# Low parts of the query units and every other quad's second ones by GpSimd; the first half of the selection under the query projection

## What is computed

```python
def peer(x, w_query, sub_keys, expert_down, expert_up):
    ...
    q = (xt @ w_query).reshape(T, PEER_HEADS, 2, PEER_HALF)
    scores = jnp.einsum('thpc,hpnc->thpn', q, sub_keys).astype(jnp.float32)
    vals, idx = lax.top_k(scores, PEER_TOPK)
    cand = (vals[..., 0, :, None] + vals[..., 1, None, :]).reshape(T, PEER_HEADS, PEER_TOPK * PEER_TOPK)
    top_vals, top_c = lax.top_k(cand, PEER_TOPK)
    i1 = jnp.take_along_axis(idx[..., 0, :], top_c // PEER_TOPK, axis=-1)
    i2 = jnp.take_along_axis(idx[..., 1, :], top_c % PEER_TOPK, axis=-1)
    experts = (i1 * PEER_N_KEYS + i2).reshape(T, PEER_HEADS * PEER_TOPK)
    ...
        u = jnp.take(expert_down, ec, axis=0)
        hdn = jax.nn.gelu(jnp.einsum('ted,td->te', u, xc))
        vsel = jnp.take(expert_up, ec, axis=0)
        return jnp.einsum('te,ted->td', gc * hdn, vsel)
```

## Time and profile before

| | us |
|---|---|
| median of 3 runs | 2942.48 (2939.5 to 2945.15) |
| profiled execution | 2936.86 |
| its span | 2935.1 |
| PE busy | 2811.8 (96%) |
| DVE busy | 2050.6 (70%) |
| ACT busy | 1118.3 (38%) |
| POOL busy | 542.0 (18%) |

### The profile page before, as it was taken

One profiled execution on the slowest core, in us unless ns is written; L12 is line 12 of the kernel. 1 busy time (PEld: TensorE's weight loads), 2 busy tenths in 40 slices (PEclk: granted clock), 3 DMA queues, 4 the chain that ended last, 5 costly groups with the idle time before them and its releaser, 6 DMA issues.

```text
span 2935.1 us, 40591 instructions
## 1 busy us (share of the span) xinstructions
PE 2811.8 (96%) x15985; PEld 2275.7 (78%) x15985; DVE 2050.6 (70%) x3115; ACT 1118.3 (38%) x1743; POOL 542.0 (18%) x534
## 2 busy tenths in 40 slices
PE   6999999999999999899999999999999989999997
PEld 4788888887879988798897799888888877444443
DVE  4688877778765456744655669985559999666666
ACT  3344444445454445644455542112027986000000
POOL 1000000000000000000000002334435457544443
PEclk9999999999999999999999999999999999999999
DMA  9988888887866635365443646999998888999997
GB/s 362 361 288 271 270 269 269 270 268 269 294 201 179 174 112 167 124 201 170 136 130 122 202 135 231 351 339 409 407 356 284 295 295 322 408 409 409 409 409 319
DMA packets 345757, 799.55 MB, mean 272 GB/s; under 512 B 40104, under 2 KB 95648, under 8 KB 344800
## 3 DMA queue, kind: packets, MB, share of 16 engines
q1 hardware_dynamic: 270576, 505.70, 50.6%
q0 software_dynamic: 74992, 291.27, 26.4%
HBM read 794.76 MB, written 2.10 MB: 271 GB/s over the span
## 4 chain that ended last, share of the span: by engine, by line
PE 67%; DMA 14%; DVE 6%; ACT 5%; issue 4%; POOL 4%; SPq 0%; DVEq 0%; ACTq 0%; POOLq 0%
PE ps L2042 16%; PE ps L2044 15%; PE ps L2043 15%; PE ps L2607 13%; DMA s<-in_up_rows,s 12%; POOL s L735 3%; DVE s L1995 2%; DVE r L1268 1%; ACT s L1185 1%; DMA s<-in_down_rows,s 1%; DMA s<-in_ret_first 1%; DVE s L1976 1%; ACT s L1155 1%; ACT s L1163 1%; PE ps L2342 1%
## 5 line engine op out<-in xcount | busy, mean ns | idle before, releaser
L2042 PE MATMUL ps<-r,r 128*128 128x256 f32 (+1 forms) x2976 | 999.9, 336 | 14.8 <-DVE r L1268 12.4
L2044 PE MATMUL ps<-r,r 128*128 128x256 f32 (+1 forms) x2976 | 980.1, 329 | 0.0
L2043 PE MATMUL ps<-r,r 128*128 128x256 f32 (+1 forms) x2976 | 979.3, 329 | 0.0
L1268 DVE TENSOR_TENSOR r<-s,r 128x1024 fp32r<-128x1024 f32 (+2 forms) x532 | 640.1, 1212 | 418.9 <-ACT r L750 417.0
L750 ACT CAST r<-s 128x1024 fp32r<-128x1024 f32 (+2 forms) x532 | 549.0, 1039 | 740.2 <-PE ps L2044 696.8
L2042 PEld LDWEIGHTS ps<-r,r 128*128 128x128 f32 x2976 | 569.0, 191 | 81.0 <-issue 21.2
L2043 PEld LDWEIGHTS ps<-r,r 128*128 128x128 f32 x2976 | 569.3, 191 | 52.6 <-issue 5.3
L2044 PEld LDWEIGHTS ps<-r,r 128*128 128x128 f32 x2976 | 568.3, 191 | 50.5
L2732 PE MATMUL ps<-s,big 128*128 128x512 f32 x1024 | 441.6, 594 | 1.5 <-DMA s<-in_up_blocks 1.5
L1995 DVE SCALAR_TENSOR_TENSOR s<-s,s,s 128x1024 f32<-128x1024 f32 x256 | 328.8, 1284 | 162.3 <-DMA s<-in_up_rows,s 160.6
L1976 DVE CUSTOM_DVE_ANT_0 s<-s,s 128x1152 f32<-128x1152 f32 x256 | 345.6, 1352 | 97.3 <-DMA s<-in_down_rows,s 97.1
(11 more groups left out here) (315 smaller groups left out, 2244.1 us busy)
## 6 DMA issues: line engine op xcount, KB each, us to landing
s<-in_ada_w SPq DMA_DIRECT2D x128, 512.0 KB, 5.5
s<-in_up_blocks SPq DMA_DIRECT2D x128, 512.0 KB
s<-in_ret_w_in SPq DMA_DIRECT2D x112, 512.0 KB, 5.3
s<-in_down_blocks SPq DMA_DIRECT2D x128, 448.0 KB
s<-in_w_in SPq DMA_DIRECT2D x96, 512.0 KB, 3.9
s<-in_ret_w_out SPq DMA_DIRECT2D x64, 512.0 KB, 5.8
s<-in_ret_w_in SPq DMA_DIRECT2D x112, 256.0 KB, 4.1
s<-in_mla_w_in SPq DMA_DIRECT2D x48, 512.0 KB, 3.9
```

Of the source, the lines that this page charges most:

```text
L1268: v.tensor_tensor(lo_of(w), raw_of(w), hi_of(w).bitcast(F), ALU.subtract).then_inc(*lo_made.to(w))
L2042: pe.matmul(o, lh, rh, start=start, stop=False, skip_group_check=True)
L2043: pe.matmul(o, lh, rl, start=False, stop=False, skip_group_check=True)
L2044: return pe.matmul(o, ll, rh, start=False, stop=stop, skip_group_check=True)
```

## The change

- **Low parts.** Of the 32 query units, 10 to 31 get their low part from GpSimd (`POOL_LO`, semaphore `lo_pool`); DVE skips them.
- **Selection.** `both` now runs the top-16 lists of groups 0 and 1 of both tiles first (`best`), then the combining halves of f = 0, then the rest tile by tile. The list values of tile 1 have buffers of their own for that (`VAL1`, `IDX1`). 148 of the 292 steps stand behind unit 9's step, without subtractions between them, and ahead of the first row; three instead of four go ahead of each row.
- **Rings and picks.** The ring of seven serves rows 0 to 61. The first tile's picks stand at rows 157 to 188, one per row; the second tile's stay.
- **Ones.** In the first tile's build, for odd quads (`by_pool`): ACT makes the first ones without the coefficient from PE's `compare` (one activation of 128x512 in place of four of 128x128, then the same one as before), and GpSimd makes the second ones times coefficient, four tensor_scalars of 128x128, into a new buffer `OHG` (`pool_ones`, semaphore `pool_hot`). DVE has no `first_ones` there. In POOL's queue the four stand ahead of the gather of row 195 + 2q, and wait for the build of quad q - 2. `OHG` lies on the place of up block 129, which waits for the last build of the tile.
- Three DMA semaphores are joined into one.

```diff
@@ -18,7 +18,7 @@
-RINGS = ((0, 7), (56, 4), (256, 6), (320, 7))
+RINGS = ((0, 7), (62, 4), (256, 6), (320, 7))
@@ -265,6 +265,7 @@
         VAL, IDX, IDF = scratch(16, 16)[0], scratch(16, 16)[0], scratch(16, 16)[0]
+        VAL1, IDX1 = scratch(8, 16)[0], scratch(8, 16)[0]
@@ -305,6 +306,12 @@
+        OHG = at(W + 6144, 4, 128)
+        def by_pool(t, q):
+            return t == 0 and q % 2 == 1
@@ -494,13 +501,19 @@
         hi_made = sig("hi_made", range(NW))
-        lo_made = sig("lo_made", range(NW))
+        POOL_LO = range(PQW + 10, NW)
+        lo_made = sig("lo_made", [w for w in range(NW) if w not in POOL_LO])
+        lo_pool = sig("lo_pool", POOL_LO)
+        def lo_ready(w):
+            return (lo_pool if w in POOL_LO else lo_made).at(w)
@@ -602,7 +615,7 @@
         multiplied, picked = sig("multiplied", fours), sig("picked", fours)
-        first_hot = sig("first_hot", fours)
+        first_hot, pool_hot = sig("first_hot", [x for x in fours if not by_pool(*x)]), sig("pool_hot", [x for x in fours if by_pool(*x)])
@@ -654,9 +667,11 @@
-        PICK_AT = [150 + 6 * q // 5 for q in range(32)] + [189 + 2 * q for q in range(32)]
+        PICK_AT = [157 + q for q in range(32)] + [189 + 2 * q for q in range(32)]
...
+        ONES_AT = {min(195 + 2 * q, 255): q for q in range(1, 32, 2)}
@@ -668,7 +683,7 @@
                     elif plan[o][0] == "w":
-                        sp.wait_ge(*lo_made.at(w_of[o]))
+                        sp.wait_ge(*lo_ready(w_of[o]))
@@ -684,6 +699,8 @@
                     sp.wait_ge(*block_used.at(127))
+                if b == 129:
+                    sp.wait_ge(*built.at((0, 31)))
@@ -714,12 +731,29 @@
+            for w in POOL_LO:
+                g.wait_ge(*hi_made.at(w))
+                g.tensor_tensor(lo_of(w), raw_of(w), hi_of(w).bitcast(F), ALU.subtract).then_inc(*lo_pool.to(w))
+            def pool_ones(q):
+                if q == 1:
+                    g.wait_ge(*block_used.at(127))
+                    g.wait_ge(*coef_copied.at(0))
+                else:
+                    g.wait_ge(*built.at((0, q - 2)))
+                for k in range(4):
+                    c = 4 * q + k
+                    r = g.tensor_scalar(OHG[:, k, :], LESS.bitcast(F), SECOND[0][:, c:c + 1], CFT[0][:, c:c + 1],
+                                        ALU.is_equal, ALU.mult)
+                r.then_inc(*pool_hot.to((0, q)))
@@ -728,6 +762,8 @@
                     g.wait_ge(*gate_in.at(1))
+                if n in ONES_AT:
+                    pool_ones(ONES_AT[n])
@@ -1180,9 +1216,14 @@
                         s.wait_ge(*built.at((0, q - 1)))
-                    for k in range(4):
-                        c = 4 * q + k
-                        r = s.activation(o2[:, k, :], STEP, ACT.Abs, bias=SECOND[0][:, c:c + 1])
+                    if by_pool(0, q):
+                        o2 = OH1[0]
+                        s.wait_ge(*compared.at((0, q)))
+                        r = s.activation(flat(o2), bank[0], ACT.Abs)
+                    else:
+                        for k in range(4):
+                            c = 4 * q + k
+                            r = s.activation(o2[:, k, :], STEP, ACT.Abs, bias=SECOND[0][:, c:c + 1])
@@ -1262,7 +1303,7 @@
                         ada(i, *plan[i][3])
-                    elif plan[i][0] == "w":
+                    elif plan[i][0] == "w" and w_of[i] not in POOL_LO:
@@ -1854,16 +1895,26 @@
+            def tops(t, f):
+                a = slice(8 * f, 8 * f + 8)
+                return (VAL1, IDX1) if (t, f) == (1, 0) else (VAL[:, a, :], IDX[:, a, :])
+            def best(t, g):
+                val, idx = tops(t, g // 2)
+                v.wait_ge(*sel_copied.at((t, g)))
+                for j in range(4):
+                    hp, i = 4 * g + j, 4 * (g % 2) + j
+                    v.wait_ge(*steps.at())
+                    yield from top16(SC[t][:, hp * 128:(hp + 1) * 128], val[:, i, :], idx[:, i, :].bitcast(U32), WK[:, 0:128])
             def select(t, f):
-                for hp in range(8 * f, 8 * f + 8):
-                    if hp % 4 == 0:
-                        v.wait_ge(*sel_copied.at((t, hp // 4)))
-                    yield from top16(SC[t][:, hp * 128:(hp + 1) * 128], VAL[:, hp, :], IDX[:, hp, :].bitcast(U32), WK[:, 0:128])
-                    v.wait_ge(*steps.at())
                 a = slice(8 * f, 8 * f + 8)
-                V2 = VAL[:, a, :].rearrange("p (h a) k -> p h a k", a=2)
+                val, idx = tops(t, f)
+                V2 = val.rearrange("p (h a) k -> p h a k", a=2)
                 I2 = IDF[:, a, :].rearrange("p (h a) k -> p h a k", a=2)
-                v.tensor_copy(IDF[:, a, :], IDX[:, a, :].bitcast(U32)).then_inc(*steps.to())
+                v.wait_ge(*steps.at())
+                v.tensor_copy(IDF[:, a, :], idx.bitcast(U32)).then_inc(*steps.to())
@@ -1917,17 +1968,21 @@
             def both():
-                for f in range(2):
+                for g in range(2):
                     for t in range(2):
-                        yield from select(t, f)
+                        yield from best(t, g)
+                for t in range(2):
+                    yield from select(t, 0)
+                for t in range(2):
+                    for g in (2, 3):
+                        yield from best(t, g)
+                    yield from select(t, 1)
             choice = both()
-            for g in range(4):
-                for u in range(8):
-                    step(PQW + 8 * g + u)
-                    if 8 * g + u >= 10:
-                        for _ in range(4):
-                            next(choice)
+            for u in range(10):
+                step(PQW + u)
+            for _ in range(148):
+                next(choice)
@@ -1970,7 +2025,7 @@
                 if n:
-                    for _ in range(4):
+                    for _ in range(3):
@@ -1981,7 +2036,7 @@
                     coefficients(0)
-                if n in HOT_AT:
+                if n in HOT_AT and not by_pool(0, HOT_AT.index(n)):
@@ -2045,7 +2100,7 @@
-                pe.wait_ge(*lo_made.at(w))
+                pe.wait_ge(*lo_ready(w))
@@ -2665,7 +2720,7 @@
                 r = less(t, q, 0, b)
-                free[b] = first_hot.at((t, q))
+                free[b] = (less_read if by_pool(t, q) else first_hot).at((t, q))
@@ -2674,9 +2729,9 @@
                 take(b)
-                pe.wait_ge(*first_hot.at((t, q)))
+                pe.wait_ge(*(pool_hot if by_pool(t, q) else first_hot).at((t, q)))
                 pe.wait_ge(*second_hot.at((t, q)))
-                o1, o2 = (OH1[q % 2], OH2[q % 2]) if t else (OH1[0], OH2[0])
+                o1, o2 = (OH1[q % 2], OH2[q % 2]) if t else (OH1[0], OHG if by_pool(t, q) else OH2[0])
```

19 lines of the change are left out of this document (10 added, 9 removed).

## The result

The changed kernel takes **2986.74 us** (median of 4 runs, 2981.12 to 2987.79) against 2942.49 for the kernel before in the same runs (4 runs): ratio 1.0157, interval 1.0137 to 1.0177. I had said 2932.5, at most 2947, so it is 54 us above the forecast and 40 above the range. The profiled execution took 2987.66 us (span 2985.8).

What follows compares the result with a forecast made beforehand. Bound by PE and full DMA in the long stretches; savings only in 228 us where PE waits for or serves helpers. Terms 6 + 4 + 0 = 10 us off the 2942.5 median: 2932.5 us, range 2924 to 2947.

Steps and rivals of the forecast that it cites:

- Part 1, units on GpSimd: Under the query projection, GpSimd takes 22 subtractions at 2.4 us each (1.23 to 3.7); cost 0, high end 9 us.
- Part 1, the selection: Selection moved earlier: steps end about 1805, row 48 at 1932, row 157 done before the first pick at 2191.3.
- the cover: Slack before the first tile's picks: rows could lose 18 us and row 157 would still be in time.
- Part 1, the picks: First tile's 32 picks run with 32 rows instead of 38: 73.3 us for 80.6, 6 us saved (0 to 7.3).
- two side lines: Second row buffers starting at row 62 instead of 56, and block 129 waiting for the first tile's build: both costed at nothing.
- Part 2, ACT and DVE: First tile's build: ACT saves 0.59 us per odd quad, pair 7.49 instead of 8.08; DVE's share at most 7.4.
- Part 2, the four operations on GpSimd: First tile's build: four tensor_scalars at 0.3 us, together 1.2, make a pair 7.8 us; 4 us saved.
- my high end: First tile's build: 0.94 us per GpSimd operation, 3.8 per set, a pair 10.3 us, 31 us lost.
- The port: First tile's build: a set of ones could stand behind a DVE row, pair 9.1 us, 8 us lost, 2950.5.
- Rival "slower by the ring": First tile's build: ones delay their gather until the four-buffer ring passes 8.08 us; 17 lost less 6, 2953.5; chance 0.14.
- Part 3, the tail: Between the last pick and the up rows: later last gather against shorter DVE and ACT work, taken as 0 (-1 to +2).
- The gain is taken back: Rival: the DMA-full last 449 us make gathers starting 10 us earlier meet the same limit; 2942.5, chance 0.06.

Runs made afterwards that it cites:

- e7: Changed kernel without GpSimd's ones, second row buffers from row 60, wait of block 129 kept, the 22 low parts back on DVE: 2942.83 us, ratio 1.0024.
- e14: The kernel of e8 run again, on another chip: ratio 0.9962 to the kernel before.
- e8: Changed kernel without GpSimd's ones, second row buffers from row 60 instead of 62, no wait ahead of block 129: 2926.6 us against 2938.94 before.
- e1: Changed kernel with GpSimd making no ones, every quad built as before, the rest of the change kept: 2934.33 us against 2939.95 before.
- e6: Changed kernel with DVE's operation of rows 194 to 255 replaced by a plain sum with one SBUF input: 2944.13 us, ratio 1.0021 to before.
- e10: Changed kernel with each set of ones made by one GpSimd operation of 128x512 instead of four of 128x128: 2951.24 us, ratio 1.0039 to before.
- e3: Changed kernel with GpSimd's ones on every fourth quad instead of every second, 8 sets instead of 16: 2959.08 us, ratio 1.0065 to before.
- e2: Kernel before with only GpSimd's ones of every other quad added, old ring of buffers: 2998.23 us, ratio 1.0194.

## Why the prediction was wrong, point by point

- **Part 1, units on GpSimd**: right. 2.41 us for 2.4, and PE is busy 64.90 us of the 66.3 from 1729.60, as before. The Trainium skill's figure (GPSIMD Engine Reference, section 3.1) gave an estimate of 2.25; the trace says 2.41.
- **Part 1, the selection**: right. The first row at 1806.8 for a reckoned 1805, the last step that feeds a row at 1934.6 for 1932, row 157 in time with 4 us of idle DVE. e7 shows the other side of the cover: without the offload PE waits 10.1 us.
- **Part 1, the picks**: right, 73.75 us for 73.3; to the first ones 83.6 for 91.3, 7.7 us. As a whole the part gives 11 to 12 us (e14, e8), twice the 6 that I counted; about 7 of them lie between the first pick and the dense stretch, and the others single profiles can't place. That e1 came out 5.6 us faster, so near the 6, is luck: two side lines that I had at 0 held back the other half.
- **Part 2, ACT and DVE**: the saving was never reached, since neither sets the pace now; not tested.
- **Part 2, the four operations on GpSimd: the step that failed.** I took 0.3 us "because the tile is that of the 0.29 row". That row is DVE's. For the subtraction I had taken twice DVE's price and been right; here I took it once. Undisturbed it is 0.79 (14 us of build for 16 sets, e6), with the rows in the way 1.46 (53 us), where I had forecast 4 us saved. Even my high end, 0.94 each and 10.3 us a pair, was too low, because it had no wait in it: the pair takes 12.2.
- **The port.** The row that took 1.81 us instead of 0.94 showed it, and I priced it at one row (1.28 us) per set. A set has four operations, and each of them can begin beside a row: 40 of the 64 are held up and take 1.1 to 2.0 us. e10, with one operation per set, loses 0.4 us per set to rows, and not 2.5. And the gathers themselves stretch too (1.22 us).
- **Rival "slower by the ring"** had the mechanism and the point from which it decides (0.39 us each), at 2953.5, 33 us short. It deserved the place of the forecast, with the price above. e3 shows that the loss doesn't need a full queue.
- **Part 3, the tail**: taken as 0 (-1 to +2). In the trace it is 7.2 us longer. Without GpSimd's ones the ring's start makes 4 to 7 us of tail (10.3 with 60); with them it is the down rows behind the last set, since e2 has 17.2 us with the old ring. The wait of block 129, "60 us before PE reads it: 0", was judged by who needs the block and not by whom its load disturbs.
- **The gain is taken back**: no. From the first matmul of the dense stretch to the end it is 459.6 us, before 460.2; the 452.5 of the row above is only a stretch cut elsewhere.

## What to carry to other kernels

An engine that idles half of a stretch is not free if it is also the queue through which the stretch's transfers go: add up what would stand in that queue per period, at durations of that engine and not of another, before comparing with the period. Where DVE runs operations with two SBUF inputs, count how many of GpSimd's operations can begin beside one: each waits for what is left of it, here up to 1.2 us, and for the next if that follows at once. One large operation is held up once where four small ones are held up four times. A shifted ring start or a load that is held back is an edit of its own: look for the transfer that it delays or collides with, and take it out alone.
